# Expert layers of a decoder step: four experts per pass of the array instead of two and two

## The reference, cut to what matters

```
for g in range(N_GROUPS):                     # 4 groups of 8 experts, D_MODEL 1024, D_EXPERT 256
    hid = silu(einsum('nd,edf->nef', t, w_gate[g])) * einsum('nd,edf->nef', t, w_up[g])
    y = y + einsum('nef,efd->nd', hid * combine[:, g, :, None], w_down[g])
```

## Time and profile before

| | |
|---|---|
| median of 3 runs | 826.6 us (822.04 to 829.06) |
| the profiled execution | 832.18 us, its span 830.3 us |
| mean granted TensorE clock | 0.864 |
| TensorE matmul, busy | 629.7 us (76%) |
| VectorE / ScalarE / GpSimd, busy | 314.2 (38%) / 149.9 (18%) / 129.1 (16%) us |
| moved by DMA | 245.12 MB, mean 295 GB/s |
| the expert loop, first to last gate/up matmul | 529.95 to 786.46 us |

### The profile page before, as it was taken

One profiled execution on the slowest core, in us unless ns is written; L12 is line 12 of the kernel. 1 busy time (PEld: TensorE's weight loads), 2 busy tenths in 40 slices (PEclk: granted clock), 3 DMA queues, 4 the chain that ended last, 5 costly groups with the idle time before them and its releaser, 6 DMA issues.

```text
span 830.3 us, 7873 instructions
## 1 busy us (share of the span) xinstructions
PE 629.7 (76%) x3108; PEld 356.3 (43%) x3108; DVE 314.2 (38%) x490; ACT 149.9 (18%) x282; POOL 129.1 (16%) x119
## 2 busy tenths in 40 slices
PE   4969898997997898766899861586777877778710
PEld 3856764676885455325774251121222222222200
DVE  3079998987899870320230155000000000000005
ACT  2124033324104515330000100110110101101101
POOL 2434222111115352111000003100000000000020
PEclk9998899999999796987799955598998899989965
DMA  9997899588657889577789010199999999999631
GB/s 339 413 411 275 313 382 409 198 322 325 242 193 262 318 294 402 204 293 298 273 325 396 34 52 0 52 350 396 399 398 402 400 394 398 400 403 398 261 128 57
DMA packets 123916, 245.12 MB, mean 295 GB/s; under 512 B 14163, under 2 KB 86371, under 8 KB 113612
## 3 DMA queue, kind: packets, MB, share of 16 engines
q1 hardware_dynamic: 103932, 140.33, 46.0%
q0 software_dynamic: 14832, 94.98, 29.7%
q10 hardware_dynamic: 5120, 9.37, 3.1%
HBM read 232.66 MB, written 12.00 MB: 295 GB/s over the span
## 4 chain that ended last, share of the span: by engine, by line
PE 36%; SPq 23%; DVE 16%; DMA 9%; ACT 6%; issue 6%; POOL 2%; ACTq 1%; POOLq 0%; DVEq 0%
SPq L443 19%; PE PS L603 8%; PE PS L1030 5%; SPq L446 4%; DVE arena L1473 4%; PE PS L1021 4%; DVE x_rows L1477 4%; PE PS L1076 4%; PE PS L947 2%; DMA arena<-in_w_proj_b 2%; PE PS L1094 2%; DMA temp<-in_cache_k_a,page_idx 2%; PE PS L724 2%; DMA arena<-in_w_up 1%; PE PS L883 1%
## 5 line engine op out<-in xcount | busy, mean ns | idle before, releaser
L1076 PE MATMUL PS<-arena,temp 128*32 128x512 f32 x512 | 138.1, 701 | 37.4 <-DMA arena<-in_w_up 36.0
L603 PE MATMUL PS<-xT,arena 128*128 128x264 f32 x608 | 142.7, 394 | 4.6 <-ACT arena L1271 4.2
L603 PEld LDWEIGHTS PS<-xT,arena 128*128 128x128 f32 x608 | 116.2, 194 | 26.1 <-ACT arena L1271 4.8
L1877 DVE TENSOR_TENSOR temp<-PS,temp 64x256 f32<-64x256 f32 x16 | 6.8, 422 | 266.5 <-ACT temp L1390 266.5
L1076 PEld LDWEIGHTS PS<-arena,temp 128*32 128x32 f32 x512 | 39.5, 125 | 132.4 <-issue 132.4
L1473 DVE TENSOR_TENSOR arena<-arena,x_rows 128x2048 f32<-128x2048 f32 x32 | 73.0, 2283 | 28.8 <-DMA x_rows<-q_dram 28.7
L1477 DVE TENSOR_REDUCE x_rows<-arena 128x32 f32<-128x2048 f32 x32 | 73.2, 2288 | 1.1
L1094 PE MATMUL PS<-arena,temp 128*32 128x512 f32 x256 | 58.0, 594 | 12.3 <-ACT temp L1394 12.3
L503 POOL DMA_INDIRECT arena<-in_cache_k_b,unit_idx x32 | 39.5, 1234 | 147.5 <-DVE x_rows L1477 142.5
L503 POOL DMA_INDIRECT arena<-in_cache_v_b,unit_idx x32 | 37.6, 1176 | 78.4 <-PE PS L947 57.8
L503 POOL DMA_INDIRECT temp<-x_dram,slot_tok x9 | 8.6, 958 | 225.2 <-PE PS L1103 223.7
(11 more groups left out here) (319 smaller groups left out, 722.1 us busy)
## 6 DMA issues: line engine op xcount, KB each, us to landing
arena<-in_w_gate SPq DMA_DIRECT2D x32, 1024.0 KB, 11.6
arena<-in_w_up SPq DMA_DIRECT2D x32, 1024.0 KB, 12.0
arena<-in_w_down SPq DMA_DIRECT2D x32, 1024.0 KB, 11.2
arena<-in_w_in SPq DMA_DIRECT2D x9, 2048.0 KB, 11.3
temp<-in_w_out SPq DMA_DIRECT2D x1, 4096.0 KB, 15.3
y_dram<-temp ACTq DMA_DIRECT2D x8, 512.0 KB, 6.5
x_rows<-in_x_prompt SPq DMA_DIRECT2D x2, 1024.0 KB
bias_dram<-x_rows SPq DMA_DIRECT2D x1, 2048.0 KB, 18.0
```

The lines of the kernel that those rows point to most:

```text
L603: last = nc.tensor.matmul(PS[0:m, n % 2, 0:T], w[:, k, c0:c0 + m], xT[:, k, :], start=(k == 0), stop=(k == KC - 1))
L1076: last = nc.tensor.matmul(PS[k * CAP:(k + 1) * CAP, 2 + n, :], xgT[:, d, k * CAP:(k + 1) * CAP], slots[k][:, d * 2 * DE:(d + 1) * 2 * DE], ...
```

## The change

SP's loop has two steps for each quad in place of four: gate and up of all four slots, then down of all four. TensorE runs the gate/up product of four experts at once, in the four column groups, all into bank 2; then `turn`; then one transpose pair, and the down product of four experts. ScalarE and VectorE have one SiLU, one product and one copy for each quad, over 128 rows in place of 64. `s_gu`, `s_hid`, `s_hT`, `s_hTc` and `s_down` count quads in place of pairs. A clearing of `hid` ahead of the loop goes away. The gathers of tokens and the writes of results stay.

```diff
-        hidT = temp[:, 6656:6656 + 4 * CAP].rearrange("p (f n) -> p f n", f=2)
+        hidT = temp[:, 6656:6656 + 2 * QUAD].rearrange("p (f n) -> p f n", f=2)
...
             with sp.Fori(1, NQ) as i:
-                for n in range(2):
-                    sp.wait_ge(s_gu, i * 2 + (n - 1))
-                    for k in (2 * n, 2 * n + 1):
-                        gate_up(bass.ds(i * 4 + k, 1), k)
-                    sp.wait_ge(s_down, i * 2 + (n - 1))
-                    for k in (2 * n, 2 * n + 1):
-                        down(bass.ds(i * 4 + k, 1), k)
+                sp.wait_ge(s_gu, i)
+                for k in range(4):
+                    gate_up(bass.ds(i * 4 + k, 1), k)
+                sp.wait_ge(s_down, i)
+                for k in range(4):
+                    down(bass.ds(i * 4 + k, 1), k)
...
             def quad(i):
                 pe.wait_ge(s_gT, i + 1)
-                two_experts(i, 0)
-                two_experts(i, 1)
+                for k in range(4):
+                    pe.wait_ge(s_we[k], i * 32 + 32)
+                for d in range(KC):
+                    for k in range(4):
+                        last = nc.tensor.matmul(PS[k * CAP:(k + 1) * CAP, 2, :], xgT[:, d, k * CAP:(k + 1) * CAP],
+                                                slots[k][:, d * 2 * DE:(d + 1) * 2 * DE],
+                                                start=(d == 0), stop=(d == KC - 1))
+                last.then_inc(s_gu, 1)
+                if not (isinstance(i, int) and i == NQX - 1):
+                    turn(i + 1)
+
+                pe.wait_ge(s_hid, i + 1)
+                for f in range(2):
+                    last = nc.tensor.transpose(PS[:, ACC + 2, f * P:(f + 1) * P], hid[:, f * P:(f + 1) * P], ident)
+                last.then_inc(s_hT, 1)
+                pe.wait_ge(s_hTc, i + 1)
+                for k in range(4):
+                    pe.wait_ge(s_wd[k], i * 16 + 16)
+                for half in range(2):
+                    for f in range(2):
+                        for k in range(4):
+                            w0 = 16 * DE + f * D + half * 512
+                            last = nc.tensor.matmul(PS[k * CAP:(k + 1) * CAP, ACC + half, :],
+                                                    hidT[:, f, k * CAP:(k + 1) * CAP],
+                                                    slots[k][:, w0:w0 + 512], start=(f == 0), stop=(f == 1))
+                last.then_inc(s_down, 1)
...
             def quad(i):
 
-                for n in range(2):
-                    rows = slice(2 * n * CAP, 2 * (n + 1) * CAP)
-                    act.wait_ge(s_gu, i * 2 + (n + 1))
-                    nc.scalar.activation(act_e[rows, :], PS[rows, 2 + n, 0:DE], ACT.Silu).then_inc(s_act, 1)
-                    if n == 1 and not (isinstance(i, int) and i == NQX - 1):
-                        turned_tokens(i + 1)
-                    act.wait_ge(s_hT, i * 2 + (n + 1))
-                    nc.scalar.copy(hidT, PS[:, ACC + 2, 0:2 * P].rearrange("p (f m) -> p f m", f=2)[:, :, rows]
-                                   ).then_inc(s_hTc, 1)
+                act.wait_ge(s_gu, i + 1)
+                nc.scalar.activation(act_e, PS[:, 2, 0:DE], ACT.Silu).then_inc(s_act, 1)
+                if not (isinstance(i, int) and i == NQX - 1):
+                    turned_tokens(i + 1)
+                act.wait_ge(s_hT, i + 1)
+                nc.scalar.copy(hidT, PS[:, ACC + 2, 0:2 * P].rearrange("p (f m) -> p f m", f=2)).then_inc(s_hTc, 1)
                 act.wait_ge(s_yout, i * 16 + 16)
-                act.wait_ge(s_down, i * 2 + 2)
+                act.wait_ge(s_down, i + 1)
...
-                for n in range(2):
-                    rows = slice(2 * n * CAP, 2 * (n + 1) * CAP)
-                    u = PS[rows, 2 + n, DE:2 * DE]
-                    dve.wait_ge(s_act, i * 2 + (n + 1))
-                    nc.vector.tensor_tensor(hid[rows, :], u, act_e[rows, :], ALU.mult).then_inc(s_hid, 1)
-
-            link(nc.vector.memset(hid, 0.0))
+                dve.wait_ge(s_act, i + 1)
+                nc.vector.tensor_tensor(hid, PS[:, 2, DE:2 * DE], act_e, ALU.mult).then_inc(s_hid, 1)
+
```

More of the change, by code:

```diff
@@ L492, in _ @@
                 with sp.If(n_extra > 4 * q):
+                    sp.wait_ge(s_down, NQ + q)
                     for k in range(4):
                         j = 4 * q + k
-                        sp.wait_ge(s_down, NE // 2 + j // 2 - 1)
                         e = sp.value_load(ovf_i[0:1, 1 + j:2 + j], min_val=0, max_val=NE - 1)
```

## The result

The changed kernel is slower. Its median of 4 runs is 844.3 us (841.76 to 849.97) against 824.8 us of the kernel before on the same chip: ratio 1.024, 95% interval 1.017 to 1.031. A second comparison later gave 1.020 (1.015 to 1.025), 848.7 against 829.4 us. The forecast was 839 us and +12.3 us; the medians moved by +19.5 and +19.3 us, while the profiled execution took 845.56 us, 13.4 us more than that of before.

What follows compares the result with a forecast made beforehand. The prediction took the DMA stream of weights, bytes over rate, to bound the kernel. Six dry gaps (+16.8 us) and a shorter end (-4.5 us) gave +12.3 us on the 826.6 us median: 839 us, range 824 to 850 us.

Steps and rivals of the forecast that it cites:

- What bounds the kernel: Expert loop: bytes over DMA rate, 240 us at 397 GB/s; TensorE has slack, so shortening its work gives nothing by itself.
- The price of a four-group burst: TensorE gate/up: four column groups go at the price of two, 16 steps, 9.3 us assumed (8.76 to 9.83).
- six seams: Places between down loads of one quad and gate/up loads of the next, quads 1 to 6, where the queue runs dry.
- The gap: Refills between quads: 12.8 us against 10.0 us of queued loads; queue dry 2.8 us, 6 times, +16.8 us.
- restart: Refill: from the burst's end until the flow of the next gate/up loads begins in effect, 2.4 us.
- the down bytes: Four down loads left in the queue behind a quad's last gate/up load, lasting 10.0 us.
- landing: From the last gate/up byte being through to the start of the burst that waits for it, 1.1 us.
- The end: Loop tail: last down product ends 6.4 us behind the last byte in place of 10.9, -4.5 us.
- They neither fill the gap nor lengthen the down part: their bytes are in the 34.2 us already: Token gathers and result writes, issued behind the restart: no extra time beyond one quad's 34.2 us share of the stream.
- A clock that stays up: Rival at the seam: burst takes 6.9 us, gap 0.4 us, sum -4.5 us, 822 us; chance 0.10.

Runs made afterwards that it cites:

- e10: e6 with 24 additional matmuls on constants for each quad; 822.4 us, ratio 0.993 against the kernel before.
- e6: Changed kernel with gate/up loads cut in two, first halves requested mid-burst, and result write held until the next gate/up weights landed; 823.5 us, ratio 0.994.
- e1: Changed kernel with each slot's gate/up loads cut in two, the next quad's first halves requested in the middle of the burst; 830.4 us, ratio 1.000.
- e2: Changed kernel with SyncE loading pairwise in the old order, all waits for whole quads; 878.9 us, ratio 1.060.
- e7: Changed kernel itself, run again on the same chip as other follow-ups; 848.7 us, ratio 1.020 against the kernel before.
- e3: Changed kernel with 24 additional matmuls on constants behind each quad's down product, to keep the clock up; 840.5 us, ratio 1.017.
- e9: Changed kernel with result write held until the next gate/up weights landed, gate/up products of 2 of 8 chunks left out; 826.9 us, ratio 0.998.
- e8: Kernel before, with a quad's result write held until the next quad's down weights of slots 0 and 1 landed; one run, period 34.19 us.

## Why the prediction was right

- *What bounds the kernel*: right. TensorE's gate/up time was halved and nothing of it arrived in the time; and e10, with 24 more matmuls in every quad than e6, is no slower.
- *The price of a four-group burst*: right. 16 steps, 8.99 us on average over the six seams; 9.3 were assumed. One reading under it was off by one: 8.76 us stands for 12 of the 16 bursts before, not 11. The other two, which the forecast passes over here, took 7.06 us, with no wait ahead of them.
- *The gap*: right in its mechanism (e1, e2) and, in this pair of traces, nearly in size: 2.6 us for each seam against 2.8, 15.7 us against 16.8. Its terms at the first seam: restart 2.4 us as assumed; the down bytes 10.0 us; landing 1.65 us against 1.1; burst 8.5. A shorter burst and a longer landing partly cancelled here. The gather is not issued behind the restart, as I had written, but at 575.9 us, a microsecond ahead of it; the flow until 576.9 us stays below 90 GB/s all the same.
- *The end*: right. The last down product ends 805.45 us, 6.7 us behind the last byte (6.4 forecast, 10.9 before): -4.2 us against -4.5.
- *"They neither fill the gap nor lengthen the down part: their bytes are in the 34.2 us already"*: this is the sentence that failed. The bytes were counted, their rate was not. The stream lasts from 539.5 to 798.8 us, 259.3 us against 239.4: +19.9, of which the seams are 15.7. The other 4.2 us, 0.6 us a quad, are the slow stretches behind each restart (4 us at 323 to 334 GB/s in place of 386 miss 0.5 to 0.7 us). With them the loop is +15.7 us (19.9 - 4.2), 3.4 more than the +12.3 forecast. In the pair of traces the span shows only +13.4, since the first burst happened to end 2.7 us earlier in the changed one; that it stands so close to +12.3 is luck. The intervals of both comparisons hold 15.7 us (1.019), and 12.3 us (1.015) lies below the one and at the edge of the other. The medians moved by 19.5 and 19.3 us; what they have beyond the loop's 15.7 us (17.0 in e7) no profile places.
- *Rivals.* A clock that stays up was priced at 7 us of time for each microsecond of burst. e3 shows that this line does not hold: its bursts at the six seams were 1.2 us shorter than the changed kernel's on average (7.8 against 9.0), and landing and restart 1.1 us longer (4.7 against 3.6). e9 points the same way. With the clock up in five of seven bursts the ratio was 1.017, so nothing here supports the -4.5 us of that rival. The Trainium skill's fixed cost of about 2.0 us for a transfer (DMA: Bandwidth & Descriptors, anatomy of one DMA) is given there for transfers issued by GpSimd, while these loads are SyncE's, and it is less than this seam takes: landing and restart were 1.2 + 2.4 us on average.

Open: why one engine falls behind at a short seam, which one it is (the trace does not name the 16 engines), and why a restart and the write together slow the flow. What the runs show is an order: with more cover or an earlier request the period comes nearer to 34.19 us (37.3 with a request 2.6 us too late in effect, 35.9 with the write as cover, 35.3 with half refills, 34.7 with both). A shorter burst alone did not do it (37.45 in e3 against 37.30, 35.86 in e9 against 35.94).

## What to carry to other kernels

When a stream of loads is the bound, do not ask how long the compute is, ask what is left in the queue when the next request is made. Landing, the compute that frees the buffer, and the restart have to fit into that (here 1.2 + 9.0 + 2.4 us into 10.0), with some to spare; how much, these runs do not settle. Here the coarser buffers saved compute and cut the cover. An earlier release of half a buffer, and a transfer that was due anyway put at the seam, cost nothing that the runs show and brought most of the stream back (period 34.73 against 34.19 us).

## What the runs showed of the hardware that was not expected

- A DMA queue that nearly runs dry can be worse than the mean gap says: with gaps of 0.8 and 1.4 us the next one was 5.5 us (e3), and for 2 us of it a single engine was still at work (share 0.07 to 0.08).
- The same 0.5 MB write costs nothing beside a full queue (385 to 388 GB/s, e8) and goes with 321 GB/s for 4 us behind a restart in the changed kernel.
- 24 matmuls on constants in each waiting time of 22 us kept the granted clock at 2.4 GHz in 5 of 7 bursts (7.07 us each, PEclk 1.00); where 3.34 and 3.57 us of waiting were left, the bursts took 9.94 and 8.77 us (PEclk 0.71 and 0.81), and in one such case (3.36 us) still 7.07.
